# Two transformer blocks on one core: the last gated pair reloaded raw, VectorE's work between first-down evictions taken apart, one conv tap and four folds moved

## The reference

```python
D_MODEL = 1024; SEQ = 1024; D_FF = 2816; PLE_DIM = 256

def first_block(x, p, ...):            # after mixing
    h = rmsnorm(x, g_ffn[i])
    gate = causal_dwconv3(h @ w_gate[i], ffn_conv_w[i], ffn_conv_b[i])
    x = x + (jax.nn.silu(gate) * (h @ w_up[i])) @ w_down[i]
    ple_gate = jax.nn.sigmoid(rmsnorm(x, g_ple[i]) @ w_ple_gate[i])
    x = x + ple_gate * (p[i].astype(x.dtype) @ w_ple_proj[i])

def second_block(x, ...):              # after mixing
    h2 = rmsnorm_2(x, norm2_w[l])
    x = x + (jax.nn.silu(h2 @ w_gate[l]) * (h2 @ w_up[l])) @ w_down[l]

def causal_dwconv3(u, w, b):           # three taps over the tokens
    up = jnp.pad(u, ((0, 0), (CONV_K - 1, 0), (0, 0)))
    t = u.shape[1]
    return up[:, 0:t] * w[0] + up[:, 1:t + 1] * w[1] + up[:, 2:t + 2] * w[2] + b
```

## Time and profile before

| what | value |
|---|---|
| median of 3 runs | 2543.61 us (2543.17 to 2545.53) |
| the profiled execution | 2542.03 us |
| its span in the trace | 2540.7 us |
| PE busy | 2469.3 us, 97% |
| DVE busy | 1699.0 us, 67% |
| POOL busy | 1463.1 us, 58% |
| ACT busy | 1141.1 us, 45% |
| mean granted clock of PE | 0.994 |

### The profile page before, as it was taken

One profiled execution on the slowest core, in us unless ns is written; L12 is line 12 of the kernel. 1 busy time (PEld: TensorE's weight loads), 2 busy tenths in 40 slices (PEclk: granted clock), 3 DMA queues, 4 the chain that ended last, 5 costly groups with the idle time before them and its releaser, 6 DMA issues.

```text
span 2540.7 us, 35603 instructions
## 1 busy us (share of the span) xinstructions
PE 2469.3 (97%) x11970; PEld 2045.0 (80%) x11970; DVE 1699.0 (67%) x2901; ACT 1141.1 (45%) x2187; POOL 1463.1 (58%) x1162
## 2 busy tenths in 40 slices
PE   8999999999999999998999999889999999999999
PEld 6888888887888877886877887779888888887887
DVE  5337776289978879986367788867228444446987
ACT  6346663253333324444256666486234333333442
POOL 2133324457776668986525455373346666666987
PEclk9999999999999999998999999999999999999999
DMA  4254314212323236431323112221311322327452
GB/s 159 75 192 128 113 63 159 98 50 105 120 92 112 108 133 224 137 108 48 102 84 98 58 59 88 96 80 30 149 61 73 111 105 100 108 88 260 134 174 92
DMA packets 126677, 277.82 MB, mean 109 GB/s; under 512 B 11905, under 2 KB 33697, under 8 KB 126241
## 3 DMA queue, kind: packets, MB, share of 16 engines
q1 hardware_dynamic: 126496, 275.54, 31.8%
HBM read 200.00 MB, written 70.78 MB: 107 GB/s over the span
## 4 chain that ended last, share of the span: by engine, by line
PE 55%; DVE 3%; POOL 2%; issue 2%; ACT 1%; DMA 1%; SPq 0%; ACTq 0%; DVEq 0%; POOLq 0%
PE PS L787 6%; PE PS L789 5%; PE PS L788 5%; PE PS L1049 5%; PE PS L1050 5%; PE PS L1051 5%; PE PS L1085 4%; PE PS L1087 4%; PE PS L1086 4%; PE PS L1340 2%; PE PS L1320 1%; DMA XA<-spill 1%; PE PS L1019 1%; PE PS L1021 1%; PE PS L1020 1%
## 5 line engine op out<-in xcount | busy, mean ns | idle before, releaser
L787 PE MATMUL PS<-Hh,Wl 128*128 128x512 f32 x1072 | 435.9, 407 | 17.5 <-DVE Hl L1482 9.5
L789 PE MATMUL PS<-Hh,Wh 128*128 128x512 f32 x1072 | 422.1, 394 | 0.0
L788 PE MATMUL PS<-Hl,Wh 128*128 128x512 f32 x1072 | 421.8, 393 | 0.0
L3519 POOL TENSOR_TENSOR Wl<-Wr,Wh 128x512 fp32r<-128x512 f32 (+1 forms) x158 | 209.9, 1350 | 342.1 <-ACT Wh L2565 342.1
L3625 POOL TENSOR_TENSOR RG<-RW,RG 128x512 fp32r<-128x512 f32 x176 | 260.8, 1487 | 111.5 <-ACT RG L2893 111.3
L3625 POOL TENSOR_TENSOR RG<-SW,RG 128x512 fp32r<-128x512 f32 x120 | 169.8, 1415 | 178.6 <-ACT RG L2893 153.2
L1049 PE MATMUL PS<-Hh,RG 128*128 128x512 f32 x640 | 250.4, 391 | 5.1 <-DVE VW L1860 5.1
L787 PEld LDWEIGHTS PS<-Hh,Wl 128*128 128x128 f32 x1072 | 205.3, 192 | 57.4 <-POOL Wl L3519 11.3
L1050 PE MATMUL PS<-Hl,RG 128*128 128x512 f32 x640 | 249.8, 390 | 0.0
L1051 PE MATMUL PS<-Hh,RG 128*128 128x512 f32 x640 | 249.8, 390 | 0.0
L789 PEld LDWEIGHTS PS<-Hh,Wh 128*128 128x128 f32 x1072 | 203.2, 190 | 44.7
(11 more groups left out here) (443 smaller groups left out, 6071.6 us busy)
## 6 DMA issues: line engine op xcount, KB each, us to landing
hgscr<-GB SPq DMA_DIRECT2D x100, 256.0 KB, 2.0
RW<-in_wg SPq DMA_DIRECT2D x44, 512.0 KB, 3.7
RW<-in_wu SPq DMA_DIRECT2D x44, 512.0 KB, 4.6
R<-in_wd SPq DMA_DIRECT2D x40, 512.0 KB, 3.8
Wr<-in_wi SPq DMA_DIRECT2D x27, 512.0 KB, 3.4
Hl<-hgscr SPq DMA_DIRECT2D x16, 768.0 KB, 7.6
hgscr<-acc SPq DMA_DIRECT2D x40, 256.0 KB, 2.0
HC<-hgscr SPq DMA_DIRECT2D x12, 768.0 KB, 6.6
```

What stands on the lines that cost most here:

```text
L787: pe.matmul(ps(b), k.Wl[:, s, wc], xh[:, kx, sl], start=kk == 0, stop=False)
L788: pe.matmul(ps(b), k.Wh[:, s, wc], xl[:, kx, sl], start=False, stop=False)
L789: i = pe.matmul(ps(b), k.Wh[:, s, wc], xh[:, kx, sl], start=False, stop=kk == nk - 1)
L3519: i = pool.tensor_tensor(k.Wl[:, s, c], k.Wr[:, s, c], k.Wh[:, s, c].bitcast(F32), ALU.subtract)
```

## The change

1. **Order of the last pieces.** Product 2 of tile 21 moves from among the pieces of tile 20 to between products 5 and 3 of its own tile. `u` is written ahead of `sums` in a loop step.
2. **Last pair.** Pair 10 is stored as its four raw blocks (`last_store`) and reloaded raw, part 1 and part 2 with 256 KB and 512 KB in place of 768 KB each. The four differences are made in the down stage by DVE (`late_sum`), at (unit, step) (12, 6), (13, 0), (13, 6) and (14, 0). `pair_first` and `pair_rest` of this pair are gone from gate and up and from the first-down products.
3. **Pair 0** is loaded straight into its place, without `G0h`; several of SP's waits change with it, and the loads of `x` rows 5, 6 and 7 wait for fewer stores.
4. **First-down.** DVE's other operations stand one at a time between evictions.
5. **First tap of half 0** of tiles 2 to 21, first block only, goes from DVE to ACT, behind ACT's copy of the gate.
6. **Folds** of units 18 and 19 go from POOL to DVE, right ahead of the additions that wait for them.
7. **Hand-over.** `stat` moves from slots 1 and 4 to 5 and 7 of the first products; `spread` from slot 5 of these and 2 of the third product to 2 and 6 of the third. ACT and DVE have high and low parts of half 1 earlier, and squares and roots later.

```diff
-    for a in (2, NF - 2):
-        out += [(f, p) for p in (1, 2) for f in (a, a + 1)]
-        out += [(f, p) for f in (a, a + 1) for p in ((6, 7, 5, 3, 4) if f == NF - 1 else (6, 7, 5, 4, 3))]
...
+    out += [(NF - 2, 1), (NF - 1, 1), (NF - 2, 2)]
+    out += [(NF - 2, p) for p in (6, 7, 5, 4, 3)]
+    return out + [(NF - 1, p) for p in (6, 7, 5, 2, 3, 4)]
...
+LATE = NF // 2 - 1
+OPENED = {4: (1, 0), 5: (1, 3), 8: (2, 0), 9: (2, 3), 14: (1, 6), 15: (2, 6)}
+LATE_SUMS = {(12, 6): 3, (13, 0): 2, (13, 6): 1, (14, 0): 5}
...
-                    {1: lambda: stat("ple", 0), 4: lambda: stat("ple", 1), 5: lambda: spread("ple", 0)}, fresh=lo("ple"))
+                    {5: lambda: stat("ple", 0), 7: lambda: stat("ple", 1)}, fresh=lo("ple"))
...
-                {2: lambda: spread("ple", 1)} if t == 2 else (), fresh=lo("ple") if t == 2 else None)
+                {2: lambda: spread("ple", 0), 6: lambda: spread("ple", 1)} if t == 2 else (), fresh=lo("ple") if t == 2 else None)
...
-            if f >= 2:
+            if f >= 2 and half:
                 for e in k.gb_free(tag, f, half):
                     dve.wait_ge(*at(*e))
...
+            f = DUE["u"].get(n)
+            if f is not None and f not in opened:
+                u(f)
             f = DUE["sums"].get(n)
...
-                for z in range(4):
-                    down_sum(tag, 0, z)
+                down_sum(tag, 0, 0)
+                down_sum(tag, 0, 1)
             dve.wait_ge(*at("d0", tag, m, half))
             dve.wait_ge(*at("x_back", tag, m))
             dve.tensor_tensor(XA[:, m, sl], ps(b), XA[:, m, sl], ALU.add).then_inc(*up(("free", b), "xd0", tag, m, half))
-            if (m, half) == (2, 1):
-                pair_rest(NF - 1)
-            if half and m in (4, 5):
-                down_sum(tag, 1, 2 * m - 8)
-                down_sum(tag, 1, 2 * m - 7)
...
+            t = 2 * m + half
+            if t < 2:
+                down_sum(tag, 0, 2 + t)
+            if 9 < t < 14:
+                down_sum(tag, 1, t - 10)
+            if t in OPENED:
+                hg_low(tag, *OPENED[t])
...
+            if x >= NX - 2 and i in (2, 3):
+                z, p2, out = (("21", 4, x21), ("12", 3, x12))[i - 2]
...
+                dve.tensor_tensor(out, out, V, ALU.add).then_inc(*up("fold_v", "fold", tag, x, z))
...
+            if (x, i) in LATE_SUMS:
+                late_sum(tag, LATE_SUMS[x, i])
...
+    def late_sum(tag, j):
...
+        a, b = {3: (2, 0), 2: (6, 2), 1: (6, 3), 5: (4, 1)}[j]
+        out, a, b = (k.landed(LATE, i) for i in (j, a, b))
+        dve.tensor_tensor(out, a, b, ALU.subtract).then_inc(*up("t", "ht", tag, LATE, j))
...
                     act.activation(k.SG[f % 2][:, 2:514], ps(b), ACT.Copy).then_inc(*up(("free", b), "gate_raw", f))
+                    act.wait_ge(*at("gate_raw", f))
+                    for e in k.gb_free(tag, f, 0):
+                        act.wait_ge(*at(*e))
+                    act.activation(GB[:, f % 2, h0], k.SG[f % 2][:, 2:514], ACT.Identity, bias=k.col("ffn_conv_b", f),
+                                   scale=k.col("ffn_conv_w", 44 + f)).then_inc(*up("tap0", "fv", 0, f, 0))
...
-            if x >= NX - 4 and i in (2, 3):
+            if NX - 4 <= x < NX - 2 and i in (2, 3):
...
             if n == NP - 9:
-                sp.wait_ge(*at("fp", tag, NF - 1, 2))
+                sp.wait_ge(*at("fp", tag, NF - 1, 1))
```

More of the change, by code:

```diff
@@ L415, in memory @@
     k.HD, _ = put("HD", [128, 6, 2, 512], base + 24 * T, F32R)
+    k.HDr, _ = put("HDr", [128, 6, 2, 512], base + 24 * T)
     at += 16 * T
@@ L573, in blocks, with landed @@
         return (k.HC, k.HD)[z][:, j - 1:j + 2, 0, :], (k.HC, k.HD)[z][:, j - 1:j + 2, 1, :]
+    def landed(pair, j, n=1):
+        if pair == LATE and j:
+            return k.HDr[:, j - 1, 1, :] if n == 1 else k.HDr[:, j - 1:j + n - 1, 1, :]
+        return (k.block(pair, j)[1] if n == 1 else k.blocks(pair, j)[1][:, 0:n, :]).bitcast(F32)
+    k.landed = landed
     def down_raw(v):
@@ L648, in memory @@
     k.hg = nc.dram_tensor("hgscr", (NF // 2, 128, 7, 512), F32, kind="Internal").ap()
-    k.stage, k.block, k.blocks, k.raws, k.made, k.kept = stage, block, blocks, raws, made, kept
+    k.block, k.blocks, k.raws, k.made, k.kept = block, blocks, raws, made, kept
     k.down_src, k.down_piece, k.hd, k.pair_parts = down_src, down_piece, k.acc[:, 0:512], pair_parts
@@ L1931, in feed_forward @@
                 sums(tag, f)
-            f = DUE["u"].get(n)
-            if f is not None and f not in opened:
-                u(f)
             f = DUE["v"].get(n)
@@ L3137, in hg0_high @@
         act.wait_ge(*at("hg0_in", tag, q))
-        act.activation(k.Hh[:, 2 * q:2 * q + 2, half_of(0)], k.stage(q), ACT.Copy).then_inc(*up("hg_hi", "hg0_hi", tag, q))
+        rows, sl = slice(2 * q, 2 * q + 2), half_of(0)
+        act.activation(k.Hh[:, rows, sl], k.Hl[:, rows, sl].bitcast(F32), ACT.Copy).then_inc(*up("hg_hi", "hg0_hi", tag, q))
     def hg_high(tag, pair, part):
         act.wait_ge(*at("hg_in", tag, pair, part))
-        hi, lo = k.blocks(pair, 3 * part - 2) if part else k.block(pair, 0)
-        act.activation(hi, lo.bitcast(F32), ACT.Copy).then_inc(*up("hg_hi", "hg_hi", tag, pair, part))
+        if pair == LATE and part:
+            act.wait_ge(*at("ht", tag, pair, 5))
+        j = max(0, 3 * part - 2)
+        hi = (k.blocks(pair, j) if part else k.block(pair, 0))[0]
+        act.activation(hi, k.landed(pair, j, 3 if part else 1), ACT.Copy).then_inc(*up("hg_hi", "hg_hi", tag, pair, part))
     feed_forward("ffn", True, "ple")
@@ L4123, in feed_forward @@
                 hg_load(2, 2)
-                for q in range(2):
-                    sp.wait_ge(*at("hg0_lo", tag, q))
+                sp.wait_ge(*at("fp", tag, NF - 1, 2))
                 hg_load(1, 0)
```

106 lines of the change are left out of this document (63 added, 43 removed).

## The result

| | before | after |
|---|---|---|
| median of 4 runs | 2543.45 us (2543.17 to 2545.53) | 2518.22 us (2515.50 to 2519.79) |
| the profiled execution | 2542.03 us | 2515.50 us |
| its span | 2540.7 us | 2514.2 us |

The ratio is 0.9896, with an interval of 0.9884 to 0.9909: 25 us faster. The forecast was 2517.5 us, range 2511 to 2528.

What follows compares the result with a forecast made beforehand. PE, busy 97% of the span, bounds the kernel, so only its waits and the lower clock behind them can be won. Gains 3.3 + 9.5 + 11 + 3.3 - 1 = 26.1 us gave 2517.5 us, range 2511 to 2528.

Steps and rivals of the forecast that it cites:

- The wait at 627: First block, PE waiting 3.53 us for `v`: wait falls to 2.0 and the clock stays full, gain 3.3 us.
- End of gate and up, first-down, first block: Of 13.0 us lost to waits, half clock and restarts there, 3.5 stay: gain 9.5 us (6.5 to 12.5).
- The late tap of tile 21: ACT's copy and tap behind four high parts of down weights delay the first eviction: 2.2 us of waiting (0 to 3.5).
- the 4.3 us: PE's wait at the end of gate and up, first block: tile 21's taps stand ahead of `v` and `c22`; all 4.3 goes.
- Hand-over: From down units to per-layer stage: folds off POOL and later `stat` remove most of 13.1 us lost, gain 11.
- the walk over four engines: Hand-over's new order followed on all engines with listed durations: no long wait found, some 2 us left over.
- Second block: End of gate and up and first-down there: 4.1 us of waits go but for some restarts, gain 3.3 (2 to 4).
- Down stage: Eight late differences on DVE, with 0.86 us free per unit, cost 1 us in all (0 to 12).
- The rule on ports: Down units: DVE's folds and late differences block POOL through a shared port lock; by that 5 to 6 us lost.
- The half-mended hand-over: Rival, 18%: low parts on DVE still stand among the squares' additions; gain 6 in place of 11, 2522.5 us.
- The slower one: Rival, 3%: ACT's tap waits for its buffer and holds up casts of weights behind it; 2549 us or more.
- the sign that was named for being wrong: First block's gate and up: ACT's tap has idle time ahead of it that ends with a store.

Runs made afterwards that it cites:

- e1: Changed kernel with the first tap of half 0 back on DVE: PE's wait 3.54 us, gate and up of the first block 386.77 us against 385.7.
- e4: Changed kernel with product 2 of tile 21 back among tile 20's pieces: gate and up of the first block 390.29 us against 385.73.
- e8: Changed kernel with SP's loads of pair 4 put behind those of activation rows 6 and 7: first block's down units 191.56 us against 192.8.
- the second profile: The changed kernel itself, without edit, profiled again in a later side-by-side run: median 2518.90 us, ratio 0.9899 to the kernel before.
- e9: Changed kernel with ACT's cast of the per-layer input and GpSimd's subtraction moved behind the eighth high part: hand-over 131.30 us against 133.1.
- e5: Changed kernel with DVE's first-down operations grouped again, without the last pair's differences: first-down 24.63 and 23.08 us, 2.4 and 1.3 over the changed kernel.

## Why the prediction was right, and where it wasn't

The total came out (2517.5 against 2518.2), with the hand-over's two causes and the end of gate and up by the mechanism that was given, and the other terms off by up to 2.2 us. By its steps:

**The wait at 627, 3.3 us.** Measured 2.6 in the profile that the result came with, about 0.9 in the second. The step that failed is the one on the clock, "nothing behind waits up to 2.4, so at 2.0 I expect none": first, the wait didn't fall to 2.0 but to 2.94, since the taps behind took back 1.0 of the 1.5 us; second, the length of the wait doesn't decide whether the clock falls (3.54 us kept it in e1, and 1.8 at the hand-over lost it in six profiles of nine), so 1.6 of the 2.6 us are chance. The tap's own share is 0.6 us of wait, 1.0 of the stage (e1).

**End of gate and up, first-down, first block, 9.5.** Measured 6.1 at the wait for `c22`, 6.0 in first-down, -0.8 near 915 and -1.1 in unit 0: 10.2. The bounds held. The wait for `v` of tile 20 was foreseen (1.3, measured 1.09 where it was 0.41). The late tap of tile 21 was put at 2.2 us; the first evictions waited for nothing in this profile and made PE wait 0.3 to 0.7 us in five others. The reason given for the 4.3 us held, as far as it names the order of pieces: with the order undone the wait is 4.01 (e4), and the tap on ACT has no share in it. That the load of `XA` would come early enough was wrong: it still ended DVE's idle time, and unit 0 waited 1.1 us, since 1.8 MB for a later use stood ahead of it (e8) and its issue wasn't soon enough to bear that.

**Hand-over, 11.** Measured 9.2 in one profile and 7.9 in the other. The two causes were right (3.6 and 4.9 us). What the walk over four engines missed is GpSimd's 4.58 us beside DVE's last low parts, 1.8 us, and PE's wait of 1.6 for weights that still stand behind sums of squares: their low parts ended 2.6 us behind the start of the last down product, 6.4 before, which is 3.8 sooner and not 5. The first of these could have been read from the kernel before, whose timelines of GpSimd and of DVE have

```profile
1184.28 4.60 POOL L3719 TENSOR_TENSOR Pl<-PR,Ph 128x2048 fp32r<-128x2048 f32 x1 [7.81 <-ACT Ph L3086]
```

and

```profile
1184.85 4.58 DVE L2065 SCALAR_TENSOR_TENSOR Hl<-XA,cols,Hh 128x512 fp32r<-128x512 f32 x1 [1.61 <-ACT Hh L3105]
```

PE had no wait behind that low part; the walk took undisturbed durations.

**Second block, 3.3.** Measured 5.5 (4.5 in the second profile). This is the term that was mis-sized by its own rule: four waits add up to 4.1 us in the view, but the stages were 5.6 us over 21.75 and 380.80. The 0.2 to 0.3 us of restart beside each wait were added in the first block and forgotten in the second, a further 0.4 lay in delays too short for the view, and the 0.8 that it left standing went too.

**Down stage, -1.** The late differences cost nothing, PE having no wait in units 12 to 15; the folds, costed at nothing, took 0.9 us in the first block, since beside them DVE has low parts of the next stage. The other 1.1 of the 2.0 are unit 0's load. "0.86 us free per unit" was a mean over units, and where the four operations went there was none.

**The rule on ports.** From the Trainium skill's rule (SBUF — State Buffer, "Who interferes with whom") the prediction estimated that the sum would lose 5 to 6 us for the late differences. The measurement decides against that estimate: units 12 to 15 lost nothing by them. In the other direction the trace agrees with the rule: two of DVE's low parts took 5.70 us beside GpSimd's long subtraction, and four took 2.74 once e9 had moved it.

**The rivals.** The half-mended hand-over was nearest, with 2 to 3 us of its 5 come true. The slower one, ACT's tap waiting for its buffer, came in its beginnings only. ACT's tap did wait for a store, the sign that was named for being wrong, 2.97 us at tile 2 and 0.23 at tile 3, but PE had no wait there; at tile 4 and all later ones it runs right behind its copy.

```profile
573.06 0.82 ACT L3073 ACTIVATE GB<-SG,cols 128x512 f32<-128x512 f32 x1 [2.97 <-DMA hgscr<-GB]
...
606.35 0.58 ACT L3069 ACTIVATE SG<-PS 128x512 f32<-128x512 f32 x1
606.97 0.82 ACT L3073 ACTIVATE GB<-SG,cols 128x512 f32<-128x512 f32 x1
```

That the total was so close is in part luck: the terms came to 2.6 + 10.2 + 9.2 + 5.5 - 0.9 = 26.6 us against 26.1, with 1.8 us less in the hand-over and 2.2 more in the second block, and the profiled execution kept the clock at both places where others of the same code lost it.

## What to carry to other kernels

Cost a wait of the bottleneck by the distance between its matmuls' starts, not by the idle time in the view, and do so in every stage alike. Spare time of an engine has to be read at the place where the new work goes, and an operation taken from a busy engine gives back less than its length when another engine's accesses fall upon the next one instead. Taking operations away and taking them apart each paid here, the second on top of the first (3.6 and 2.4 us of first-down in the first block, by the kernel before, e5 and the changed one; the 3.6 hold what the order of pieces and the loads did there).
